# Broadcast rows by transposes instead of products, and products of constants in the waits of two norms

## The chip, the cores and the metric

The kernel runs on one core of one Trainium2 chip. The metric is the device time of one launch in microseconds (us); lower is better. TensorE multiplies matrices into PSUM, VectorE (DVE) and ScalarE (ACT) do the element-wise work, GpSimd (POOL) does a little of it, and SyncE (SP) issues the loads of weights.

## The reference, cut to what matters

A sequence of 512 tokens of width 1024 goes through two blocks, all in float32. The first block is a norm, a projection, banded attention beside a pooling branch, a gated mix, an output projection whose result is normed and added to `x`, and then a convolution-gated feed-forward whose result is normed and added again. The second block is a norm, a projection, four heads of a gated delta rule (chunked recurrence) beside four heads of differential attention, and an output projection.

```python
x = x + rms_norm(mix, norm_mix_post)                       # first norm with a wait
f = conv_gated_ffn(rms_norm(x, norm_ffn_pre), ...)
x = x + rms_norm(f, norm_ffn_post)                         # second norm with a wait
...
g = cumsum(g); decay = exp(where(tril, g[:, None] - g[None, :], -inf))
k_beta = k * beta;  k = k / sqrt(sum(k * k) + eps)
```

In `rms_norm` each token has one factor, and in the delta rule each token of a head has a cumulated log decay `g`, a strength `beta` and a factor of its key's norm. Each of these is a column of numbers (a token per partition) that is also needed as a row (a token per column, the same on all 128 partitions), because activations are stored with features on partitions and the 512 tokens along the free dimension.

## The kernel before, in words

Everything is hand-scheduled: each engine has one program in order, and they meet at semaphores. Weights come in 155 units of 128x1024 through a ring of four buffers. ScalarE rounds a unit to `Wh` (L1697), VectorE takes the rest `Wl` (L1023), and TensorE does three products of 128x512 for each 128x128 piece: `Wh*Hh`, `Wh*Hl`, `Wl*Hh` (L509, L510, L512, and L544 where several units run together behind a norm). These dense products are most of the kernel.

A row is made from four columns (128 tokens each) by four calls on TensorE. The operand `scalars[:, t:t+1]` is one column of four, spread with stride 0 over 128 columns, and is multiplied with the identity, so that each partition of the output gets the same 128 numbers. A float32 product of two operands is issued as two passes, each with its own weight load, so a row of four calls is 8 passes; a call of `pe.transpose` is one pass (the transposes of L753 are 4 passes for four tiles). The rows are:

- `norm_row(turn)` (L576 to L582) for the norms before the first projection (turn 0), the feed-forward (turn 1) and the second block (turn 2);
- the row in `post_norm(turn)` (L592 to L596), for the norm after the mix (turn 0) and after the feed-forward (turn 1);
- three rows for each of the four heads in TensorE's `prep` (L800 on), by `row_of` (L745): "g" and "b" (L806, L807), and "kr", the factors of the keys' norms (L827). For "g" the second operand is an upper triangular matrix in place of the identity, so that the product also cumulates the log decays `glog` of the head; "b" spreads `beta`. Both read `gs`, into which VectorE's `prep` copies them first (L1363, L1364), and TensorE waits for that copy.

`post_norm` is where TensorE waits. All units before it are done; TensorE then waits until ScalarE has squared the last sum (L1816), adds up squares over the partitions with products of one column (L588, L589), VectorE scales the sums (L1081), GpSimd takes the power -0.5 (L2115), TensorE spreads the factors as a row (L594), VectorE scales and adds the first tile of `X` (L1068, L1071), ScalarE makes its rounded part `Hh` (L1711), and VectorE the rest `Hl` (L1037). Then the dense products start again in `units_together` (L544), tile after tile of the eight: four units at once in turn 1, two at once in turn 2, where products of one column (L563) stand between the tiles.

In the second block the order is written as rounds: `second_block` runs four stages, one for each head, in which the preparation of head `a` runs beside the recurrence (`scan`) and the attention (`diff`) of the head before, and dense products of later units (3 at a time) fill in between. All engines walk through the same rounds. At the start of stages 1 to 3, TensorE does the first product of the recurrence (L887), the rows and products of `diff`, the rows "g" and "b", some dense products, and then the second products of the recurrence (L892), which read `head_VN`. VectorE makes that (L1485) behind a copy of a unit (L1023), which waits for ScalarE's rounding (L1697), which stands behind the gate function of that stage (L1889) in ScalarE's order.

Of the kernel before, what the change touches and what calls it, by code (L numbers as in the profile page):

```python
# [18 lines left out]
P = 128  # L19
# [3 lines left out]
NT = S // P  # L23
# [124 lines left out]
def program(nc, ctx, x_in, w_units, w_ba, cols_in, mats_in, rope_in, rows_in, relb_in, counts_in,  # L148
# [7 lines left out]
    def sb(name, shape, dt=F32):  # L156
        t = nc.alloc_sbuf_tensor_at(name, shape, dt, offset=place[0])
        size = 4
        for n in shape[1:]:
            size *= n  # L160
        place[0] += (size + 31) // 32 * 32
        return t
# [93 lines left out]
    St = sb("St", [P, P])  # L256
    gs = sb("gs", [P, 2, NT])
    rqk = sb("rqk", [P, 2 * NT])
# [18 lines left out]
    def steps(name, names):  # L277
        return Steps(nc, ctx, name, names)
# [18 lines left out]
    def sum_read(g):  # L297
# [75 lines left out]
        x for lv in levels for x in (("y", lv), ("t", lv), *(("kt", "qk") if lv == 1 else ()))), "u", "w"])  # L373
    prep_dv = steps("prep_vector", ["gs", "d", "bm", "dt", "ms", "vb", "kn", "lt0", "lt", "strips",
                                    "m0", "tt", "ti", "lm", *(
# [122 lines left out]
    def tensor_program():  # L498
# [77 lines left out]
        def norm_row(turn):  # L576

            pe.wait_ge(*norm_gp.at(turn, "rstd"))
            for t in range(NT):
                ins = pe.matmul(PS[:, 2, tok(t)], rstd[:, t:t + 1].to_broadcast([P, P]), ident[:],  # L580
                                start=True, stop=True)
            ins.then_inc(*norm_pe.tick(turn, "bcast"))  # L582

        def post_norm(turn):
            pe.wait_ge(square_added, (turn + 1) * KT)
            pe.wait_ge(square_done, (turn + 1) * KT)
            for t in range(NT):
                pe.matmul(PS[:, 3, t:t + 1], ssum[:, tok(t)], ones[:], start=True, stop=False)  # L588
                ins = pe.matmul(PS[:, 3, t:t + 1], sq[:, (KT - 1) % 2, tok(t)], ones[:],  # L589
                                start=False, stop=True)  # L590
            ins.then_inc(*post_pe.tick(turn, "cols"))
            pe.wait_ge(*post_gp.at(turn, "rstd"))  # L592
            for t in range(NT):
                ins = pe.matmul(PS[:, 2, tok(t)], rstd[:, t:t + 1].to_broadcast([P, P]), ident[:],  # L594
                                start=True, stop=True)
            ins.then_inc(*post_pe.tick(turn, "bcast"))  # L596

        def attention(i):
# [145 lines left out]

        def row_of(bank, scalars, rhs):  # L745
            for t in range(NT):
                ins = pe.matmul(bank[:, tok(t)], scalars[:, t:t + 1].to_broadcast([P, P]), rhs,
                                start=True, stop=True)
            return ins
# [50 lines left out]
        def prep(st, i):  # L800
            yield
            pe.wait_ge(*prep_dv.at(i, "gs"))
            if i:
                pe.wait_ge(*prep_ac.at(i - 1, "u"))
                pe.wait_ge(*prep_dv.at(i - 1, "wt"))
            row_of(b6, gs[:, 0, :], mat(K_UPPER)).then_inc(*prep_pe.tick(i, "g"))  # L806
            row_of(b7, gs[:, 1, :], ident[:]).then_inc(*prep_pe.tick(i, "b"))  # L807
            yield
# [17 lines left out]
            pe.wait_ge(*decay_ac.at(i, "dt"))  # L826
            row_of(b6, rqk[:, 0:NT], ident[:]).then_inc(*prep_pe.tick(i, "kr"))  # L827
            yield
# [185 lines left out]
    def vector_program():  # L1014
# [344 lines left out]
        def prep(st, i):  # L1359
            dv.wait_ge(*gate_dv.at(0, "beta_eg"))  # L1360
            if i:
                dv.wait_ge(*prep_pe.at(i - 1, "w"))
            dv.tensor_copy(gs[:, 0, :], glog[:, i, :])  # L1363
            dv.tensor_copy(gs[:, 1, :], beta[:, i, :]).then_inc(*prep_dv.tick(i, "gs"))  # L1364
            yield
# [977 lines left out]
```

## Time and profile before

| | |
|---|---|
| median of 3 runs | 1120.34 us |
| the three runs | 1119.86, 1120.34, 1129.06 us |
| the profiled execution, its own time | 1117.23 us |
| its span in the trace | 1115.8 us |
| TensorE busy with products | 1071.8 us, 96% |
| VectorE, ScalarE, GpSimd busy | 649.7, 443.1, 89.8 us |
| TensorE's mean granted clock | 0.983 of full speed |

The profiled execution's span leaves 1.4 us of its own time outside (launch and end). "Idle before" in a row is the time in which the engine had nothing, and the arrow names what ended it. The granted clock has two levels, 1.0 (2.4 GHz) and 0.5 (1.2 GHz); a figure between them is a mean over the stretch.

### The profile page before, as it was taken

What the parts mean: (1) busy time and instruction counts of PE and PEld (TensorE: products, weight loads), DVE (VectorE), ACT (ScalarE), POOL (GpSimd) and SP (SyncE); (2) the same over time, 40 slices, a digit from 0 to 9 for tenths busy, and PEclk for the clock granted to TensorE, in tenths of its full rate; (3) what the DMA queues carried; (4) which work ended last, traced back from release to release, by engine and by line L of the source; (5) the groups of instructions that cost most, each with busy time, mean ns of one, the idle gap of its engine ahead of it and who ended that gap; (6) DMA issues with size and microseconds to landing.
All of it is one profiled execution on the core that took longest, in us unless ns stands there. A gap on an engine that the chain in (4) does not pass through costs nothing.

```text
span 1115.8 us, 15447 instructions
## 1 busy us (share of the span) xinstructions
PE 1071.8 (96%) x6280; PEld 850.5 (76%) x6280; DVE 649.7 (58%) x1126; ACT 443.1 (40%) x773; POOL 89.8 (8%) x76
## 2 busy tenths in 40 slices
PE   7999999999989999999999999889999999998898
PEld 5777777778768888888888888768777777775776
DVE  6645454656337788777772212654576576575474
ACT  6233232344443544444442222434254354353431
POOL 1000000000210000000000000000120120221210
PEclk9999999999989999999999999899999999998899
DMA  8221313122331233333323233122111111111102
GB/s 328 78 89 59 95 57 95 57 76 83 106 94 57 95 113 103 105 95 96 95 93 105 85 114 113 43 73 73 59 53 44 58 57 40 57 38 40 38 19 76
DMA packets 25430, 90.80 MB, mean 81 GB/s; under 512 B 2880, under 2 KB 3136, under 8 KB 25232
## 3 DMA queue, kind: packets, MB, share of 16 engines
q1 hardware_dynamic: 23328, 83.90, 23.7%
q0 software_dynamic: 592, 3.61, 0.8%
q10 hardware_dynamic: 1440, 2.31, 0.6%
q8 instruction: 50, 0.82, 0.3%
q14 instruction: 20, 0.16, 0.0%
HBM read 87.71 MB, written 2.10 MB: 80 GB/s over the span
## 4 chain that ended last, share of the span: by engine, by line
PE 86%; DVE 7%; ACT 3%; issue 2%; POOL 1%; DMA 1%; SPq 0%; ACTq 0%; DVEq 0%; POOLq 0%
PE PS L509 22%; PE PS L512 21%; PE PS L510 21%; PE PS L544 4%; PE PS L758 1%; DVE Wl L1023 1%; PE PS L629 1%; PE PS L996 1%; PE PS L993 1%; PE PS L994 1%; PE PS L642 1%; ACT Wh L1697 1%; DVE Yc L1062 1%; PE PS L940 1%; PE PS L652 1%
## 5 line engine op out<-in xcount | busy, mean ns | idle before, releaser
L509 PE MATMUL PS<-Hh,Wh 128*128 128x512 f32 x856 | 352.0, 411 | 0.6 <-ACT M L1817 0.6
L512 PE MATMUL PS<-Hh,Wl 128*128 128x512 f32 x856 | 336.2, 393 | 0.0
L510 PE MATMUL PS<-Hl,Wh 128*128 128x512 f32 x856 | 336.0, 392 | 0.0
L1023 DVE TENSOR_TENSOR Wl<-raw,Wh 128x1024 fp32r<-128x1024 f32 x155 | 188.9, 1224 | 186.4 <-ACT Wh L1697 184.8
L509 PEld LDWEIGHTS PS<-Hh,Wh 128*128 128x128 f32 x856 | 161.7, 189 | 43.7 <-issue 11.0
L1697 ACT ACTIVATE Wh<-raw 128x1024 fp32r<-128x1024 f32 x155 | 161.4, 1051 | 72.8 <-PE PS L512 60.9
L512 PEld LDWEIGHTS PS<-Hh,Wl 128*128 128x128 f32 x856 | 161.9, 189 | 35.5
L510 PEld LDWEIGHTS PS<-Hl,Wh 128*128 128x128 f32 x856 | 162.2, 190 | 30.2 <-issue 1.4
L509 PE MATMUL PS<-Ah,Wh 128*128 128x512 f32 x176 | 69.8, 396 | 0.0
L510 PE MATMUL PS<-Al,Wh 128*128 128x512 f32 x176 | 69.8, 396 | 0.0
L512 PE MATMUL PS<-Ah,Wl 128*128 128x512 f32 x176 | 69.8, 396 | 0.0
L1816 ACT ACTIVATE sq<-PS 128x512 f32<-128x512 f32 x16 | 9.6, 598 | 88.7 <-PE PS L512 88.7
L544 PE MATMUL PS<-Hh,Wh 128*128 128x512 f32 x72 | 31.8, 442 | 12.4 <-ACT Hh L1711 12.1
L1062 DVE TENSOR_TENSOR tmp<-PS,RB 128x512 f32<-128x512 f32 x44 | 30.3, 691 | 21.1 <-PE PS L512 18.9
L1844 ACT ACTIVATE conv<-conv 128x512 f32<-128x512 f32 x22 | 13.9, 633 | 71.0 <-DVE conv L1265 71.0
L2107 POOL MEMSET ssum<- 128x512 f32 x2 | 1.1, 530 | 482.4 <-DVE Hl L1250 256.0
L512 PEld LDWEIGHTS PS<-Ah,Wl 128*128 128x128 f32 x176 | 33.1, 188 | 8.1
L510 PEld LDWEIGHTS PS<-Al,Wh 128*128 128x128 f32 x176 | 33.1, 188 | 8.1
L509 PEld LDWEIGHTS PS<-Ah,Wh 128*128 128x128 f32 x176 | 33.1, 188 | 8.1
L1831 ACT ACTIVATE conv<-tmp,cols 128x512 f32<-128x512 f32 x44 | 35.2, 802 | 6.0 <-DVE tmp L1062 6.0
L1768 ACT ACTIVATE sq<-sq,nmax 128x512 f32<-128x512 f32 (+3 forms) x32 | 17.7, 554 | 44.8 <-DVE nmax L1188 44.2
L1579 DVE SCALAR_TENSOR_TENSOR C<-Yc,cols,C 128x511 f32<-128x511 f32 (+2 forms) x36 | 26.6, 746 | 12.8 <-ACT C L2023 8.1
(313 smaller groups left out, 1508.6 us busy)
## 6 DMA issues: line engine op xcount, KB each, us to landing
raw<-in_w_units SPq DMA_DIRECT2D x155, 512.0 KB, 3.5
relb<-in_rel POOLq DMA_DIRECT2D x1, 2048.0 KB, 9.5
out<-X ACTq DMA_DIRECT2D x8, 256.0 KB, 2.1
X<-in_x SPq DMA_DIRECT2D x3, 512.0 KB, 8.0
X<-in_x SPq DMA_DIRECT2D x2, 256.0 KB, 4.3
raw<-in_w_units SPq DMA_DIRECT2D x2, 256.0 KB, 4.6
rope<-in_rope POOLq DMA_DIRECT2D x1, 512.0 KB, 4.3
mats<-in_mats POOLq DMA_DIRECT2D x1, 448.0 KB, 3.6
```

The costliest lines, as they stand in the source:

```text
L509: pe.matmul(bank, Wh[:, s, w], rhs[0](r), start=first and j == 0, stop=False)
L510: pe.matmul(bank, Wh[:, s, w], rhs[1](r), start=False, stop=False)
L512: ins = pe.matmul(bank, Wl[:, s, w], rhs[0](r), start=False, stop=last and end)
L544: return pe.matmul(banks[u], w[:, s, own], h[:, k, :], **ends)
L629: pe.matmul(PS[:, 2 + a, 0:nk], Q2[r, tok(qt)], K2[r, 0:nk], start=True, stop=True).then_inc(*att_pe.tick(i, ("scores", n, a)))
L1023: dv.tensor_tensor(Wl[:, s, :], raw[:, s, :], Wh[:, s, :].bitcast(F32), sub).then_inc(unit_split, 1)
L1062: return dv.tensor_tensor(dst, PS[:, bank_of[g], :], RB[:], mult).then_inc(bank_read[g % 2], 1)
L1579: dv.scalar_tensor_tensor(out=c[:, 3 - n:], in0=y[:, 0:S - 3 + n], scalar=col(C_CONV2 + a * 12 + 4 * j + n), in1=c[:, 3 - n:], op0=mult, o ...
L1697: ac.activation(Wh[:, s, :], raw[:, s, :], ACT.Copy).then_inc(unit_rounded, 1)
L1768: ac.activation(w, w, ACT.Exp, bias=nmax[:, b + a:b + a + 1], scale=1.0, accum_out=rsum[:, b + a:b + a + 1]).then_inc(*att_ac.tick(i, ("ex ...
L1831: ac.activation(conv[:, p % 2, j % 2, :], tmp[:, j % 2, :], ACT.Identity, bias=col(C_CONV + 4 * j + 3), scale=col(C_CONV + 4 * j + 2)).the ...
L1844: ac.activation(c, c, ACT.Gelu_apprx_tanh).then_inc(up_gelu, 1)
```

## The change

Five places change. (1) The row in `norm_row` and in `post_norm` is made by `pe.transpose` of the spread column. (2) `row_of` does the same, for all three rows of a head; "g" now reads `gcum`, the cumulated decays that VectorE already has (L1351), and "b" reads `beta` directly. (3) VectorE no longer copies into `gs`, and `gs` and its step are gone; TensorE waits for `beta_eg`, the last step of the gate chain, which runs once before the first head. (4) A new function `keep_awake(n)` issues `n` products of the identity with 256 columns of `cols`, both constants in float32, into bank 5, which nothing reads. (5) `post_norm` calls it three times: 1 product ahead of the wait for the squares, 2 ahead of the wait for the factors, and 5 behind the row.

```diff
-    gs = sb("gs", [P, 2, NT])
...
         def norm_row(turn):
             pe.wait_ge(*norm_gp.at(turn, "rstd"))
             for t in range(NT):
-                ins = pe.matmul(PS[:, 2, tok(t)], rstd[:, t:t + 1].to_broadcast([P, P]), ident[:],
-                                start=True, stop=True)
+                ins = pe.transpose(PS[:, 2, tok(t)], rstd[:, t:t + 1].to_broadcast([P, P]), ident[:])
...
+        def keep_awake(n):
+            for _ in range(n):
+                pe.matmul(PS[:, 5, 0:2 * P], ident[:], cols[:, 0:2 * P], start=True, stop=True)
...
         def post_norm(turn):
+            keep_awake(1)
             pe.wait_ge(square_added, (turn + 1) * KT)
...
             ins.then_inc(*post_pe.tick(turn, "cols"))
+            keep_awake(2)
             pe.wait_ge(*post_gp.at(turn, "rstd"))
             for t in range(NT):
-                ins = pe.matmul(PS[:, 2, tok(t)], rstd[:, t:t + 1].to_broadcast([P, P]), ident[:],
-                                start=True, stop=True)
+                ins = pe.transpose(PS[:, 2, tok(t)], rstd[:, t:t + 1].to_broadcast([P, P]), ident[:])
             ins.then_inc(*post_pe.tick(turn, "bcast"))
+            keep_awake(5)
...
-        def row_of(bank, scalars, rhs):
+        def row_of(bank, columns):
             for t in range(NT):
-                ins = pe.matmul(bank[:, tok(t)], scalars[:, t:t + 1].to_broadcast([P, P]), rhs,
-                                start=True, stop=True)
+                ins = pe.transpose(bank[:, tok(t)], columns[:, t:t + 1].to_broadcast([P, P]), ident[:])
...
-            pe.wait_ge(*prep_dv.at(i, "gs"))
+            pe.wait_ge(*gate_dv.at(0, "beta_eg"))
             if i:
                 pe.wait_ge(*prep_ac.at(i - 1, "u"))
                 pe.wait_ge(*prep_dv.at(i - 1, "wt"))
-            row_of(b6, gs[:, 0, :], mat(K_UPPER)).then_inc(*prep_pe.tick(i, "g"))
-            row_of(b7, gs[:, 1, :], ident[:]).then_inc(*prep_pe.tick(i, "b"))
+            row_of(b6, gcum[:, i, :]).then_inc(*prep_pe.tick(i, "g"))
+            row_of(b7, beta[:, i, :]).then_inc(*prep_pe.tick(i, "b"))
...
-            row_of(b6, rqk[:, 0:NT], ident[:]).then_inc(*prep_pe.tick(i, "kr"))
+            row_of(b6, rqk[:, 0:NT]).then_inc(*prep_pe.tick(i, "kr"))
...
         def prep(st, i):
-            dv.wait_ge(*gate_dv.at(0, "beta_eg"))
-            if i:
-                dv.wait_ge(*prep_pe.at(i - 1, "w"))
-            dv.tensor_copy(gs[:, 0, :], glog[:, i, :])
-            dv.tensor_copy(gs[:, 1, :], beta[:, i, :]).then_inc(*prep_dv.tick(i, "gs"))
             yield
```

## Rows read from the trace of the kernel before

**Rows 1.** The page: the span, TensorE's busy time, and the chain by engine.

```profile
span 1115.8 us, 15447 instructions
...
PE 86%; DVE 7%; ACT 3%; issue 2%; POOL 1%; DMA 1%; SPq 0%; ACTq 0%; DVEq 0%; POOLq 0%
```

**Rows 2.** Timeline, first norm's wait: start us, duration us, engine, line, operation [idle before].

```profile
324.93 0.35 PE L588 MATMUL PS<-ones,ssum 128*128 128x1 f32 x2 [0.78 <-ACT sq L1816]
...
328.21 1.25 PE L594 MATMUL PS<-ident,rstd 128*128 128x128 f32 x8 [1.36 <-POOL rstd L2115]
...
331.92 0.76 PE L544 MATMUL PS<-Hh,Wh 128*128 128x512 f32 x1 [2.46 <-ACT Hh L1711]
...
335.27 0.75 DVE L1037 SCALAR_TENSOR_TENSOR Hl<-X,cols,Hh 128x512 fp32r<-128x512 f32 x1
...
338.02 0.39 PE L544 MATMUL PS<-Hh,Wh 128*128 128x512 f32 x1
```

**Rows 3.** Windows there: us, busy PE PEld DVE ACT POOL, granted clock, DMA.

```profile
326.00:330.00 4.00, 2.10 (x16) 1.73 (x15) 0.66 (x2) 0.31 (x1) 1.02 (x1) 0.89 0.15 61
330.00:335.00 5.00, 3.08 (x7) 2.48 (x8) 4.89 (x8) 2.48 (x4) 0.00 (x0) 0.50 0.00 0
335.00:340.00 5.00, 5.00 (x21) 4.05 (x20) 4.93 (x9) 3.13 (x6) 0.00 (x0) 0.90 0.34 105
```

**Rows 4.** Timeline, second norm's wait.

```profile
703.46 2.08 PE L594 MATMUL PS<-ident,rstd 128*128 128x128 f32 x8 [1.37 <-POOL rstd L2115]
...
708.00 0.76 PE L544 MATMUL PS<-Hh,Wh 128*128 128x512 f32 x1 [2.46 <-ACT Hh L1711]
...
710.33 0.72 ACT L1711 ACTIVATE Hh<-X,cols 128x512 fp32r<-128x512 f32 x1 [0.74 <-DVE X L1071]
...
711.86 0.48 PE L544 MATMUL PS<-Hh,Wh 128*128 128x512 f32 x1
```

**Rows 5.** Windows of the second norm's wait, columns as above.

```profile
700.00:705.00 5.00, 3.63 (x23) 3.54 (x23) 0.16 (x1) 0.24 (x1) 2.04 (x3) 0.62 0.59 210
705.00:710.00 5.00, 2.54 (x8) 1.89 (x8) 4.32 (x7) 2.48 (x4) 0.00 (x0) 0.50 0.00 0
710.00:715.00 5.00, 5.00 (x29) 4.41 (x28) 4.93 (x9) 3.18 (x6) 0.00 (x0) 0.86 0.00 0
```

**Rows 6.** Timeline of TensorE, head 0: four transposes, then a row of products.

```profile
765.89 0.66 PE L753 MATMUL PS<-ident,C 128*128 128x128 f32 x4 [0.16 <-DVE rqk L1382]
766.30 0.48 PE L509 MATMUL PS<-Hh,Wh 128*128 128x512 f32 x1
...
767.78 1.05 PE L747 MATMUL PS<-ident,rqk 128*128 128x128 f32 x8
768.59 0.47 PE L509 MATMUL PS<-Hh,Wh 128*128 128x512 f32 x1
```

**Rows 7.** Timeline at the starts of stages 1, 2 and 3 (heads 1 to 3).

```profile
816.71 0.49 PE L892 MATMUL PS<-head_VN,head_Kd 128*128 128x128 f32 x2 [0.37 <-DVE head_VN L1485]
...
897.40 0.49 PE L892 MATMUL PS<-head_VN,head_Kd 128*128 128x128 f32 x2
...
974.21 1.24 DVE L1363 COPY gs<-glog 128x4 f32<-128x4 f32 x1
...
975.57 1.16 PE L747 MATMUL PS<-mats,gs 128*128 128x128 f32 x8 [0.77 <-DVE gs L1364]
975.78 1.04 ACT L1697 ACTIVATE Wh<-raw 128x1024 fp32r<-128x1024 f32 x1
...
976.85 1.23 DVE L1023 TENSOR_TENSOR Wl<-raw,Wh 128x1024 fp32r<-128x1024 f32 x1 [1.34 <-ACT Wh L1697]
...
978.99 0.49 PE L892 MATMUL PS<-head_VN,head_Kd 128*128 128x128 f32 x2 [0.66 <-DVE head_VN L1485]
```

**Rows 8.** Window of a later stretch with a wait, columns as above.

```profile
1014.00:1020.00 6.00, 3.45 (x77) 2.69 (x78) 3.95 (x13) 1.45 (x7) 0.00 (x0) 0.89 0.00 0
```

**Rows 9.** Timeline in that stretch, TensorE.

```profile
1019.39 0.48 PE L946 MATMUL PS<-ident,head_Wd 128*128 128x128 f32 x1 [2.11 <-DVE head_Wd L1563]
```

More of the change, by code:

```diff
@@ L373, in program @@
         x for lv in levels for x in (("y", lv), ("t", lv), *(("kt", "qk") if lv == 1 else ()))), "u", "w"])
-    prep_dv = steps("prep_vector", ["gs", "d", "bm", "dt", "ms", "vb", "kn", "lt0", "lt", "strips",
+    prep_dv = steps("prep_vector", ["d", "bm", "dt", "ms", "vb", "kn", "lt0", "lt", "strips",
                                     "m0", "tt", "ti", "lm", *(
```

## The prediction

> **What bounds the kernel now.** I read the page first. The reader is to see that the chain which ended last runs through TensorE for 86% of the span [rows 1]: what is taken off TensorE's own program counts in full wherever nothing else is waited for. So I read the timeline at each place that the change touches, for the wait that ends last there, and the windows of the granted clock.
>
> There are two kinds of place. At the two norms with a wait, TensorE stands idle for 0.78, 1.36 and 2.46 us in one passage [rows 2], and the clock falls: it is 0.89 in the window from 326 to 330, 0.50 in the next and 0.90 in the next [rows 3]. So it was at 1.2 GHz for 0.22 x 4 + 5 + 0.2 x 5 = 6.9 us. In the second norm the means are 0.62, 0.50 and 0.86 [rows 5], which is 3.8 + 5 + 1.4 = 10.2 us. The dense products that follow start in that state. At the rows of the second block there is no such passage. There the question is whether TensorE or the chain ScalarE, VectorE is late.
>
> **The change, part by part.** The unit of price is a row. Eight passes take 768.59 - 767.78 = 0.81 us from start to start, four transposes of the same size 766.30 - 765.89 = 0.41 us [rows 6]. A row turned into transposes gives 0.40 us at full clock.
>
> *Rows of the three norms with `norm_row`:* 3 x 0.40 = 1.2 us. VectorE waits for each of these rows, so its reading starts earlier too. I see no wait behind them that another engine alone sets.
>
> *Head 0, rows "g", "b", "kr":* 3 x 0.40 = 1.2 us. The copies into `gs` are not waited for there.
>
> *Row "kr" of heads 1 to 3:* 3 x 0.40 = 1.2 us. It lies on the chain that ended last; if the waits behind it are set by others it is worth nothing, so the bounds are 0 and 1.2, and I take 1.2.
>
> *Rows "g" and "b" of heads 1 to 3, and the copies into `gs`:* here most of the work that is removed is removed from in front of a wait. In head 3 TensorE idles 0.77 us for `gs` at 975.57, whose first copy took 1.24 us; the same in head 2. Then it idles 0.66 us at L892 for `head_VN`. That is made behind ScalarE's rounding at 975.78, and behind VectorE's split at 976.85, which had waited 1.34 us for that rounding [rows 7]. Neither waited for the rows or for `gs`. So L892 stays at 978.99 against the start of the stage, and 0.77 + 0.80 us turn into a wait there. In head 1 L892 had 0.37 us of idle already, and in head 2 it started without one, at 897.40 [rows 7], right behind the vector operation that it reads. Of 2.4 us in rows and about 1.5 us in waits for `gs`, I count 0.1 us. If I am wrong on who is late, up to 3.9 us more are gained.
>
> *The row in `post_norm`:* in the first norm 8 passes took 1.25 us and in the second, with the clock down, 2.08 us [rows 2, 4]. Four transposes take 0.66 us with their latency [rows 6], or twice that cold: 0.6 us gained in the first; in the second 1.0 us when the clock is down as before, 1.4 us when it is up. All that VectorE does for the first tile shifts by as much.
>
> *The products of constants.* The trace before has none. One has two passes of 256 columns, thus 512 columns where the 8 passes of a row have 1024: half of 0.81, or 0.41 us at full clock and 0.82 at half. One product lies in an idle time of 0.78 us; two are 0.82 us in 1.36; five are 2.05 us in 2.46 [rows 2]. All fit at full clock and cost nothing. At half clock the two take 1.64 us and the five 4.1 us: 0.3 + 1.6 = 1.9 us beyond the waits that cover them. Bounds of their own cost: 0 to 1.9 us for each norm.
>
> *What the clock gives, if it stays up.* First norm: the products of L544 before 338.02 start at 331.92 - 0.6 = 331.3. Tile 0 has 6 and tile 1 has 12 of them, 0.23 us each, thus 4.1 us if nothing is waited for, but the last four need the `Hl` that ends at 336.02 [rows 2], now 335.4. So they end at 335.4 + 4 x 0.23 = 336.3 in place of 338.02, which gives 1.7 us with the row's 0.6. From there TensorE is the late one (5.00 of 5.00 us busy [rows 3]). Second norm: tile 1 waits for `Hh`, ready at 710.33 + 0.72 = 711.05, and its products start at 711.86 [rows 4]. At full clock they start when it is ready, 0.8 us earlier, and 1.4 with the row: 2.2 us; a little more, 0.25, since the last of the sums (L588, L589) ran cold as well: 2.5 us.
>
> Will it stay up? The products fill 3.3 of some 7 us in each passage; of the rest nearly half goes to products of one column. That is near the edge: at 1018 the clock fell (0.89 over the window of rows 8, down at its end) in a stretch that ends in 2.11 us of idle, with much small work ahead of it [rows 8, 9]. I expect that it holds in some executions and norms and falls in others, but comes back sooner, as the five products are dense work behind the row. Between the row alone (0.6 and 1.0) and the whole (1.7 and 2.5) I take the middle, 1.2 and 1.8 us.
>
> By the Trainium skill, "TensorE: Matmul & The Clock Gate", section "Terms", a transpose of float32 is four times as fast; the trace has twice (0.81 against 0.41 us [rows 6]), and the sum goes by that. By the factor four, 0.2 us more would go for each of the rows that I count.
>
> *A cost.* In head 3 TensorE now idles longer in front of L892: 0.66 + 0.77 + 0.80 = 2.2 us, with transposes ahead of it. A fall of the clock there would be partly hidden, since TensorE waits for VectorE around it. I put 0.3 us to it as a mean.
>
> The sum: 1.2 + 1.2 + 1.2 + 0.1 + 1.2 + 1.8 - 0.3 = 6.4 us. Against the profiled execution (span 1115.8, its own time 1117.23) that is 1110.8; but that execution is 3.1 us below the median shown and the clock differs from one execution to the next, so I set the sum against the median: 1120.34 - 6.4 = 1113.9 us.
>
> **The rivals.** *The clock falls in both norms all the same.* Then the constants overrun at half clock. For it: the fall in rows 8 and 9. Against it: nothing in the passage is now idle for more than about a microsecond. Each norm then has its row (0.6 and 1.0) less 1.9 us, plus an earlier return of the clock, which gives 0.5 to 1.5 us: about zero. What is left is 1.2 + 1.2 + 1.2 + 0.1 = 3.7: 1116.6 us.
>
> *All works.* The clock holds in both norms (1.7 + 2.5) and no fall is added: 3.7 + 4.2 = 7.9 us, 1112.4 us. With something of the 3.9 us in front of L892 it would come below 1109.
>
> *The rows of the second block are worth nothing*, as ScalarE and VectorE set its pace: only the norms count, 1.2 + 1.2 + 1.8 = 4.2 us, 1116.1 us. For it: the waits of rows 7. Against it: 86% of the chain on TensorE [rows 1].
>
> *Slower: the rows no longer hold the clock in the second block.* At the start of stages 1 to 3 dense float32 products of two passes become transposes, and the waits at L892 grow to 0.37 + 0.8 = 1.2 us, about 1.6 and 2.2 us. If the clock falls in each of them for as long as in the norms (6.9 to 10.2 us, half of which is lost: 3.4 to 5.1 us), that costs 10 to 15 us against a gain of 6.7 without the mean cost above: 1124 to 1129, say 1126. It decides from the second such fall on. Against it: at L892 dense products follow at once, and part of the loss is hidden by VectorE. The Trainium skill says in "TensorE: Matmul & The Clock Gate", section "Part 4: PE-mode transpose", that a transpose does not count as busy for the clock in the way that a product does, which is this mechanism; no row here shows it, since transposes are always among products before.
>
> **How the numbers follow.** Forecast 1113.9: 0.50, its own range 1110.5 to 1117. The clock falls in both norms: 0.20. All works: 0.12, a third of it under 1109. Rows of the second block worth nothing: 0.12. Slower: 0.06. A measurement of this kernel tells about 1% from no change, so faster means below 1109.1 and slower above 1131.5. The tail of the forecast under 1109.1 holds 0.05, all works 0.04 and luck with the falls late in the span (rows 8) 0.02: faster 0.11. Slower than 1131.5 needs the last rival at its dearest: 0.02. The range that holds 8 in 10 is 1108 to 1119.5.
>
> **What would show it.** L594 has 4 instructions for each norm and L747 only 48, at 0.41 us a row. The granted clock in the windows of rows 3 and 5 is at or near 1.0, and L544 starts some 7.1 us behind the last product ahead of the norm, not 8.1. No `gs`; L747 is not waited for, and L892 is idle for more than a microsecond in heads 1 and 3. Wrong would be: L544 starting right behind the last constant product with the clock at 0.5 (overrun); L892 without a longer wait (then more is gained); or a clock under 1.0 between 815 and 985.

## The result, and the profile after

| | before | changed |
|---|---|---|
| median, executions | 1120.34 us, 14 | 1113.45 us, 14 |
| lowest to highest | 1117.13 to 1129.21 | 1110.31 to 1117.39 |
| profiled execution, own time (span) | 1117.23 (1115.8) | 1111.07 (1109.6) |
| mean granted clock of that execution | 0.983 | 0.986 |

The ratio of the times is 0.9905, with a 95% interval of 0.9881 to 0.9929. It stands for 10.6 us, and the means differ by 9.8 us; the medians differ by 6.9 us only, since 5 of the 14 executions of the kernel before took 1128.5 us or more and a median passes them over. The forecast was 1113.9 us and "within 1%"; both came out. The change did what it says: L599, the row in the wait of a norm, has 8 instructions where L594 had 16, the rows of the heads have 48 (L753) where L747 had 96, and `gs` is gone.

The page of the changed kernel, for [rows 1]:

```profile
span 1109.6 us, 15364 instructions
...
PE 86%; DVE 7%; ACT 3%; issue 2%; POOL 1%; DMA 0%; ACTq 0%; DVEq 0%; POOLq 0%
```

The first norm's wait in the timeline of the changed kernel, for [rows 2]; L592, L599 and L543 are L588, L594 and L544 of before, and L585 is the products of constants:

```profile
323.52 0.60 PE L585 MATMUL PS<-cols,ident 128*128 128x256 f32 x2
324.47 0.35 PE L592 MATMUL PS<-ones,ssum 128*128 128x1 f32 x2 [0.34 <-ACT sq L1816]
...
326.24 1.75 PE L585 MATMUL PS<-cols,ident 128*128 128x256 f32 x4
327.79 1.06 PE L599 MATMUL PS<-ident,rstd 128*128 128x128 f32 x4
328.65 2.99 PE L585 MATMUL PS<-cols,ident 128*128 128x256 f32 x10
331.32 0.54 PE L543 MATMUL PS<-Hh,Wh 128*128 128x512 f32 x1
...
335.47 1.19 PE L543 MATMUL PS<-Hl,Wh 128*128 128x512 f32 x4 [0.54 <-DVE Hl L1042]
336.50 0.39 PE L543 MATMUL PS<-Hh,Wh 128*128 128x512 f32 x1
```

And the second norm's, for [rows 4]:

```profile
699.60 1.11 PE L585 MATMUL PS<-cols,ident 128*128 128x256 f32 x4
701.12 0.65 PE L599 MATMUL PS<-ident,rstd 128*128 128x128 f32 x4 [0.40 <-POOL rstd L2115]
701.60 2.32 PE L585 MATMUL PS<-cols,ident 128*128 128x256 f32 x10
704.23 0.47 PE L543 MATMUL PS<-Hh,Wh 128*128 128x512 f32 x1 [0.30 <-ACT Hh L1711]
...
706.64 0.47 PE L543 MATMUL PS<-Hh,Wh 128*128 128x512 f32 x1
```

Windows of both passages in the changed kernel (us, busy PE PEld DVE ACT POOL, granted clock, DMA), for [rows 3, 5]:

```profile
324.00:328.00 4.00, 3.66 (x22) 2.98 (x22) 0.16 (x1) 1.85 (x3) 1.02 (x1) 0.82 0.48 182
328.00:332.00 4.00, 4.00 (x17) 3.45 (x17) 3.04 (x5) 1.57 (x3) 0.00 (x0) 0.75 0.00 0
332.00:336.00 4.00, 3.46 (x15) 2.41 (x14) 3.97 (x6) 2.12 (x4) 0.00 (x0) 1.00 0.39 98
698.00:702.00 4.00, 3.60 (x26) 3.12 (x26) 0.36 (x2) 0.26 (x1) 2.06 (x3) 1.00 0.78 260
702.00:706.00 4.00, 3.70 (x18) 2.67 (x17) 3.90 (x7) 2.49 (x4) 0.00 (x0) 1.00 0.01 2
```

The reader is to see two outcomes of the same remedy in one execution. In the second norm the clock stays at its upper level, and the idle times of 1.37 and 2.46 us have shrunk to 0.40 and 0.30. In the first it still fell, for about 3.4 us (0.82 and 0.75 in two windows of 4 us), so the constants there took 1.75 and 2.99 us in the records; but it was back for the dense products at L543, where before it stayed down 6.9 us. The row there was made with the clock down: it took 1.06 us where the eight passes had taken 1.25, so of the 0.6 us that the row was to give there came 0.1, and the rest of the gain is dense products at the upper level.

Where the 6.2 us came from can be read by laying marks of both traces side by side:

| mark | before | changed | ahead by |
|---|---|---|---|
| first product | 7.16 | 7.87 | -0.7 |
| sums of the first norm (L588, now L592) | 324.93 | 324.47 | 0.5 |
| its tile 1 done (L544, now L543) | 338.02 | 336.50 | 1.5 |
| sums of the second norm | 699.81 | 697.83 | 2.0 |
| its tile 1 begins | 711.86 | 706.64 | 5.2 |
| gate sums (L740, now L745) | 749.81 | 744.09 | 5.7 |
| transposes of head 0 (L753, now L758) | 765.89 | 759.26 | 6.6 |
| L892, now L897, of head 3's stage | 978.99 | 972.35 | 6.6 |
| L786, now L791 | 1007.36 | 1002.38 | 5.0 |
| first L892, now L897, of the last stage | 1055.64 | 1049.53 | 6.1 |

The late first product was made up by 15 us (both kernels then stand at 15.2), so ahead of the first norm only the row of `norm_row(0)` counts, with 0.5 us. The first norm gave 1.0 us and the second 3.2. From head 1 on the lead doesn't grow any more, but it moves:

- each "kr" row of heads 1 to 3 adds 0.4 to 0.6 us (the lead behind it is 7.2 at 835, 6.7 at 916 and 5.0 at 995 us of the kernel before, from 6.7, 6.3 and 4.4);
- rows "g" and "b" and the copies add 0.8 to 2.0 us, and the wait at L897 behind them takes it all back, to within 0.2 us;
- two falls of the clock that the profile of before doesn't have take back 1.0 us (865.9 to 869.3) and 2.2 us (971.7 to 978.5);
- one that both have is shorter in the changed kernel (3.4 us from 1016.1, against 6.8 from 1018.6), which gives 1.2 us.

The waits at L897 (changed kernel, timeline of TensorE at the starts of stages 1 to 3, for [rows 7]):

```profile
809.99 0.49 PE L897 MATMUL PS<-head_VN,head_Kd 128*128 128x128 f32 x2 [1.27 <-DVE head_VN L1485]
...
891.12 0.49 PE L897 MATMUL PS<-head_VN,head_Kd 128*128 128x128 f32 x2 [1.93 <-DVE head_VN L1485]
...
970.09 0.58 ACT L1979 ACTIVATE head_Vdt<-PS 128x512 f32<-128x512 f32 x1
970.21 1.23 DVE L1028 TENSOR_TENSOR Wl<-raw,Wh 128x1024 fp32r<-128x1024 f32 x1 [2.56 <-ACT Wh L1697]
...
972.35 0.80 PE L897 MATMUL PS<-head_VN,head_Kd 128*128 128x128 f32 x2 [2.62 <-DVE head_VN L1485]
```

and the window around the last of them, with the clock at 0.64 on average:

```profile
970.00:976.00 6.00, 3.65 (x10) 2.52 (x11) 5.79 (x9) 2.54 (x4) 1.47 (x2) 0.64 0.31 90
```

VectorE waits 2.56 us for ScalarE's rounding where it waited 1.34 after the copy into `gs`: the rows and the copies were in front of a wait that ScalarE sets. In stage 3 the longer wait of 2.62 us ends with the clock down, and the lead drops from 6.6 to 4.4 us, of which the "kr" row behind it brings 0.6 back.

### The profile page after: what moved, and what is told of

It reads as the page before. It is cut to its first block, busy times and chain, and to the rows that moved or that the text cites. A ratio compares the mean times of both kernels' runs of the same rounds, so it can differ in the third digit from the quotient of the medians.

```text
span 1109.6 us, 15364 instructions
## 1 busy us (share of the span) xinstructions
PE 1070.1 (96%) x6244; PEld 847.8 (76%) x6244; DVE 647.2 (58%) x1118; ACT 443.1 (40%) x773; POOL 89.3 (8%) x76
## 4 chain that ended last, share of the span: by engine, by line
PE 86%; DVE 7%; ACT 3%; issue 2%; POOL 1%; DMA 0%; ACTq 0%; DVEq 0%; POOLq 0%
PE PS L508 22%; PE PS L511 21%; PE PS L509 21%; PE PS L543 5%; PE PS L763 1%; PE PS L634 1%; DVE Wl L1028 1%; PE PS L1001 1%; PE PS L998 1%; PE PS L999 1%; PE PS L647 1%; ACT Wh L1697 1%; PE PS L945 1%; DVE Yc L1067 1%; PE PS L657 1%
## 5 line engine op out<-in xcount | busy, mean ns | idle before, releaser
L543 PE MATMUL PS<-Hh,Wh 128*128 128x512 f32 x72 | 30.1, 418 | 8.2 <-DVE Wl L1133 7.9
```

Of the source, the lines that this page charges most:

```text
L543: return pe.matmul(banks[u], w[:, s, own], h[:, k, :], **ends)
```

## The experiments

Every kernel was timed beside executions of the kernel before on the same chip. The mean granted clock of each execution is given with the times, since it explains most of what follows. A table of 92 executions of the kernel before, all those that ran beside e1, e5, e9 and e12, shows what it is worth:

| mean granted clock | 0.971 | 0.974 | 0.976 | 0.979 | 0.980 | 0.983 | 0.985 |
|---|---|---|---|---|---|---|---|
| executions | 17 | 14 | 4 | 22 | 16 | 6 | 2 |
| mean time, us | 1128.8 | 1126.3 | 1124.7 | 1121.5 | 1120.0 | 1117.0 | 1115.3 |

(The other eleven lie at 0.973, 0.977 and 0.982.) From 0.985 to 0.971 the time at the lower level grows by 0.014 x 2 x 1120 = 31 us and the execution by 13.5 us: 0.43 us for each cold microsecond, or 0.96 us for each 0.001 of the mean. At one clock the executions lie within 2.5 us of each other, against 14.7 us over all, so the spread of this kernel's times goes with the clock. Between two kernels the same table says less, because it matters where the cold time lies: a cold microsecond inside a wait costs little. In the profile of e2, the norms had 10.2 us less of it than in the profile of before (3.4 and 3.4 against 6.8 and 10.2), and that gave 0.1 us in the first and 1.7 in the second.

### e1 and e2: each half of the change alone

e1 leaves out the constants of the changed kernel, e2 adds the constants alone to the kernel before.

```diff
 # e1, on the changed kernel
-            keep_awake(1)
...
-            keep_awake(2)
...
-            keep_awake(5)
```

> The changed kernel without its three calls of products of constants; the rows stay transposes. Theory A (the sum of the prediction, with the second norm's part corrected by the profile after to 3.2 us where the clock holds): the rows outside the two waits give 3.7 us, the rows in the waits 0.6 and 1.0, together 5.3; with one fall of the clock early in stage 3 about 1 us is given back, so 1116 us (ratio 0.996), with the granted clock at 0.5 behind both norms and L543 starting with 0.76 us products. Theory B (the constants do nothing for the time, the clock returns anyway): the same time as the changed kernel, 1113.5 (0.994). Theory C (only the clock mattered, the rows of the second block are worth nothing): 1118 to 1120.

> The kernel before with the products of constants added in the two waits, rows still of two passes. Theory A: 1.1 us in the first norm and about 2.2 us in the second where the clock holds, a little over half of it on average: 1118 us (0.998), no fall or a shorter one in the two norms. Theory B (constants are idle work): 1120.3 (1.000). Theory C (clock is the whole gain): 1115 (0.995). With e1: the two gains should add up to that of the change.

Measured: e1 1122.05 us, ratio 0.9999 (0.9974 to 1.0023); e2 1116.17 us, 0.9955 (0.9925 to 0.9984). The rows alone gave nothing, where 4 us were expected; the constants alone 5 us, 3 more than expected; together 0.9905. The two halves don't add. The clocks say how: the mean over the executions was 0.9729 in e1 and 0.9780 in the kernel before beside it. By the table 0.005 is 4.9 us, just what the rows should have gained; and at the same clock, 0.976, e1 took about 1119.8 us (2 executions) where the kernel before took 1124.7. So the rows take some 5 us of work off, as the terms of the prediction had it (3.7 + 0.6 + 1.0 = 5.3), and in e1 the lower clock took it back. With the constants it is the other way round: at the same clock, 0.985, e2 took 1117.7 us (2 executions) and the kernel before 1115.3, and at 0.983 it was 1119.7 (1) and 1117.0 (6). So e2 is faster by its higher clock alone (a mean of 0.986), and 2.4 to 2.7 us go back, as cold time that was cheap, or as constants that are not wholly covered. The second is seen in its profile: the clock fell ahead of the first norm's row, and tile 0 began at 332.94 right behind the last constant, 0.8 us later against the sums than before (timeline of e2; in the kernel before tile 0 began at 331.92 [rows 2]):

```profile
325.13 0.35 PE L594 MATMUL PS<-ones,ssum 128*128 128x1 f32 x2 [0.34 <-ACT sq L1824]
...
330.27 2.86 PE L587 MATMUL PS<-cols,ident 128*128 128x256 f32 x10
332.94 0.47 PE L544 MATMUL PS<-Hh,Wh 128*128 128x512 f32 x1
```

The clearest view of what the constants do comes from the falls of the clock at the two norms, counted over all profiles but that of e6:

| kernels | norms with a fall | how long the clock was down at each |
|---|---|---|
| no constants: before, e1, e5, e9, e10 | 10 of 10 | 6.8 to 10.2 us in the first norm, 10.2 to 20.5 in the second |
| all constants (e8 as transposes): changed, e2, e3, e4, e8, e11, e12 | 9 of 14 | 3.4 us |
| the five behind the row alone: e7 | 2 of 2 | 3.4 and 6.8 us |

So in none of these seven profiles do they keep the clock up in both norms, but where it falls it is back when the dense products begin.

One of the two longest is in e1, in these windows behind its second norm.

```profile
698.00:702.00 4.00, 1.98 (x17) 1.86 (x16) 0.16 (x1) 1.18 (x2) 2.63 (x4) 0.90 0.51 168
702.00:706.00 4.00, 1.40 (x5) 1.03 (x6) 2.64 (x5) 1.24 (x2) 0.08 (x1) 0.50 0.23 94
706.00:710.00 4.00, 4.00 (x15) 3.42 (x14) 3.93 (x8) 2.48 (x4) 0.00 (x0) 0.50 0.00 0
710.00:714.00 4.00, 4.00 (x14) 3.42 (x15) 3.93 (x7) 2.48 (x4) 0.00 (x0) 0.50 0.00 0
714.00:718.00 4.00, 4.00 (x14) 3.42 (x14) 3.93 (x7) 2.50 (x5) 0.00 (x0) 0.50 0.00 0
718.00:722.00 4.00, 4.00 (x16) 3.42 (x16) 3.16 (x4) 3.12 (x4) 0.00 (x0) 0.54 0.00 0
```

TensorE is busy in 4.00 of 4.00 us and still at 0.50. It stayed there from 701.2 to 721.7, 20.5 us. The timeline of e1 shows what it was busy with (L562 is the sums of squares, one column each):

```profile
708.41 1.70 PE L562 MATMUL PS<-ones,up_squares 128*128 128x1 f32 x8
709.97 0.77 PE L543 MATMUL PS<-Hh,Wh 128*128 128x512 f32 x1
...
712.68 1.70 PE L562 MATMUL PS<-ones,up_squares 128*128 128x1 f32 x8
714.24 0.77 PE L543 MATMUL PS<-Hh,Wh 128*128 128x512 f32 x1
```

A tile takes 714.24 - 709.97 = 4.27 us here; warm, in the changed kernel, it takes 2.28. Each tile done cold costs 2 us, and with this mixture of six dense products and eight of one column the clock didn't come back for nearly four tiles. The same mixture doesn't always do so: in the profile of before it was back at 711.4, 3.4 us behind the start of tile 0 [rows 4, 5].

### e3 and e4: the wait in front of L897

e3 makes rows "g" and "b" of heads 1 to 3 by products again; e4 puts constants into that wait.

```diff
 # e4, on the changed kernel (TensorE's prep)
+            for _ in range((0, 4, 7, 10)[i]):
+                pe.matmul(b6[:, 0:P], ident[:], cols[:, 0:P], start=True, stop=True)
             row_of(b6, gcum[:, i, :]).then_inc(*prep_pe.tick(i, "g"))
```

> The changed kernel with rows g and b of heads 1 to 3 made by products of two passes again (6 rows, 0.40 us each, 2.4 us of TensorE's time). Theory A: they lie in front of a wait that VectorE and ScalarE set, so the idle time at L897 (1.27, 1.93 and 2.62 us in the profile of the changed kernel) shrinks by 0.8 each and the time stays: within 0.5 us of the changed kernel (1113.5). If the longer idle time is what makes the clock fall in stage 3, it may even be 0.5 to 1 us faster. Rival: the rows are on the path, 2.4 us slower, 1115.9.

> The changed kernel with 4, 7 and 10 products of constants of 128 columns (0.2 us each) ahead of row g in heads 1, 2 and 3, so that TensorE no longer idles at L897. Theory A (the idle time in front of L897 lets the clock fall in stage 3, which cost 1.7 us in the profile of the changed kernel): no fall at that place in any profile, 1 to 1.5 us faster than the changed kernel, 1112.2. Rival D (that fall is hidden by VectorE or hits anyway): same as the changed kernel, 1113.5. Rival E (the constants delay the rows, which VectorE waits for): slower by up to 1 us.

Measured: e3 1114.03 us, 0.9915 (0.9880 to 0.9950); e4 1113.83 us, 0.9907 (0.9870 to 0.9944), both as the changed kernel. The intervals alone are too wide for the 2.4 us of TensorE's work that e3 puts back (that of e3 spans 8 us), but its timeline shows where it goes. Laid beside the changed kernel, e3 falls behind by 0.9 to 1.0 us at the two rows of each head and has made it up at L904, to within 0.02 us in all three heads. So that the six rows lie in front of a wait that others set is shown. The idle time moved as told (timeline of e3, heads 2 and 3; L904 is L897):

```profile
895.94 0.49 PE L904 MATMUL PS<-head_VN,head_Kd 128*128 128x128 f32 x2 [1.03 <-DVE head_VN L1492]
...
977.18 0.49 PE L904 MATMUL PS<-head_VN,head_Kd 128*128 128x128 f32 x2 [1.71 <-DVE head_VN L1492]
```

Neither profile has a fall at that place, but the medians did not move by the 1 to 1.5 us that I gave to it. Both have other falls that the changed kernel lacks (3.4 us at 724 and 6.8 at 772), so a fall that is gone in one place is not a gain over many executions; how often the one in stage 3 happens is not known.

### e5 and e6: the sums of one column moved

```diff
 # units_together, for the last norm
-                if squares is not None and m < KT:
-                    pe.wait_ge(*norm_sq.at(turn, m))
...
+            if squares is not None:
+                pe.wait_ge(*norm_sq.at(turn, KT - 1))
+                for m in range(KT):
+                    for t in range(NT):
...
```

> The kernel of e1 (rows transposed, no constants) with the 32 sums of squares of the last norm (one column each, L562) moved from between the tiles of units_together behind the last tile; the same instructions, another order. Theory F (behind the second norm the clock stays down for tile after tile, 20.5 us in the profile of e1, because products of one column lie between the tiles; a cold tile takes 4.3 us and a warm one 2.3): the clock comes back within two windows of about 5 us of the first dense products, and the time falls by 4 to 6 us against e1, to 1117 (ratio 0.996). Rival G (the long stretch is chance, or set by the wait alone): as e1, 1122 (1.000).

> The changed kernel with the same move of the sums. Theory F: where the constants hold the clock there is no long cold stretch left to cure, so the slower executions (1116 to 1117) go and the median falls by at most 1 us: 1113 (0.990). Rival G: no difference at all, or slower by up to 1 us, as the last sums are no longer spread.

Measured: e5 1121.18 us, 0.9992 (0.9966 to 1.0018); e6 1120.69 us, 0.9982 (0.9959 to 1.0006). (One execution of e6, the profiled one, took 1506 us at a mean clock of 0.65; it is left out of the ratio and its profile isn't used.) The time was a miss, and the mechanism isn't shown. In the profile of e5 the clock was back at 711.5 in the third tile, 10.2 us after its fall and not 20.5, as Theory F wants it. But the kernel before has its sums between the tiles, and its profile shows 10.2 us as well; e10, which is the kernel before at that place, shows 17.1. So rival G, chance, stands. What e5 does show is a new place to lose time: now all the sums stand together, and the clock falls in them (timeline of e5):

```profile
711.31 0.48 PE L543 MATMUL PS<-Hh,Wl 128*128 128x512 f32 x1
...
720.53 9.44 PE L562 MATMUL PS<-ones,up_squares 128*128 128x1 f32 x64
731.31 1.12 PE L578 MATMUL PS<-ident,rstd 128*128 128x128 f32 x4 [1.34 <-POOL rstd L2093]
```

TensorE was busy all through it. The block took 9.44 us where 64 passes took 8 x 0.81 = 6.5 between the tiles of the changed kernel. It was cold from 725.1 for another 10.2 us. Also, nothing covers this block: it stands whole between the last tile and the norm's chain. e6 shows the cost of that in the changed kernel, which had no long stretch to cure: 7 us slower by the medians (on another chip), where I expected at most 1.

### e7 and e8: which of the constants, and whether transposes do as well

```diff
 # e7: without keep_awake(1) and keep_awake(2)
 # e8, in keep_awake
-                pe.matmul(PS[:, 5, 0:2 * P], ident[:], cols[:, 0:2 * P], start=True, stop=True)
+                for t in range(4):
+                    pe.transpose(PS[:, 5, tok(t)], cols[:, 0:P], ident[:])
```

> The changed kernel with only the five products of constants behind the row; the one and the two ahead of it are left out. Theory F: the clock falls in most executions, since the waits ahead of the row are empty again, but the five are dense work that brings it back before or soon after the tiles begin: most of the gain is kept, 1115 (0.992). Rival H (the fall itself must be avoided): the five run cold (4.1 us in a wait of 2.5), the clock stays down behind the second norm as in e1, 1121 (0.999).

> The changed kernel with each product of constants (2 passes of 256 columns) replaced by four transposes of 128 columns, the same time on TensorE. If transposes count for the clock as products do: 1113.5 (0.991) and clocks as in the changed kernel. If they don't, as the Trainium skill says: the clock falls as in e1 and they run cold beside it, 1121 to 1123 (1.000).

Measured: e7 1115.02 us, 0.9935 (0.9907 to 0.9963), clocks 0.979 to 0.986, close to Theory F: the five behind the row keep 7 of the 10.6 us. In its profile the clock fell in both norms and the five ran cold, in the second for 4.28 us in the records, so tile 0 began right behind them at 705.67 without idle time; but the clock was back by then (705.7), and the tiles ran warm. The three ahead of the row were not tried alone. e8 1112.61 us, 0.9925 (0.9898 to 0.9953), clocks 0.982 to 0.988 with a mean of 0.9847, against 0.984 in the changed kernel. Transposes of constants do as well for the clock as products: in its profile too the clock held in the first norm and fell for 3.4 us in the second, as in e3 and e4. In this kernel the statement of the Trainium skill ("TensorE: Matmul & The Clock Gate", "Part 4: PE-mode transpose") that they don't count as busy in the same way is not borne out, and the measurement decides.

### e9 and e10: which rows give the gain back

e9 turns only the five rows of norms into transposes, e10 only the twelve of the heads; both on the kernel before, without constants.

> The kernel before with only the five rows of norms (L580, L594) made by transposes; the rows of the heads stay products, gs stays. e1 showed that all rows together are worth nothing without the constants, with a mean granted clock of 0.973 in every execution against 0.978 before. Theory J (it is the rows in the norms' waits that give the gain back: TensorE has less to do there, the clock falls sooner and stays down longer behind the second norm): no faster than before or slower, 1121 to 1124 (1.000 to 1.002), clock near 0.973. Theory K (it is given back in the second block): 2.8 us faster in work, 1119 (0.9975), clocks spread as before (0.971 to 0.985).

> The kernel before with only the twelve rows of the heads made by transposes and gs gone; the rows of the norms stay products, no constants. Theory J: the gain of the heads' rows is kept, 2.5 us: 1119.2 (0.998). Theory K (the longer waits at L892 make the clock fall in the second block): as before or slower, 1121.7 to 1123 (1.000 to 1.001). With e9 it shows which half gives the gain back.

Measured: e9 1120.18 us, 0.9970 (0.9946 to 0.9994), mean clock 0.9787; e10 1122.05 us, 0.9989 (0.9966 to 1.0013), mean clock 0.9754; the kernel before beside them 0.9769. Theory J isn't borne out: the rows of the norms keep their gain: 3.4 us by the ratio, and 1.9 us at the same clock, 0.979 (1119.6 us in five executions against 1121.5), for 2.8 expected. The rows of the heads at the same clock, 0.976, take 1121.6 us (eight executions), 3.1 us less than the 1124.7 of the kernel before, but the mean clock is 0.0015 lower, which is 1.4 us, and the interval includes no gain. At the same clock the halves add up, 1.9 + 3.1 = 5.0 us, as much as e1 has; it is the clock that differs. So the loss would lie more with the heads' rows, which is Theory K; but the two intervals overlap, and neither half alone has the clock of e1 (0.9729), so it may need both. Where in the span is not settled. The profiles don't tell it clearly: both have long stretches behind the second norm (20.5 us in e9, 17.1 in e10 by the granted clock), e10 one more fall at 733.9, at a row that it did not change, and the last fall is 13.7 us long in e10, 10.2 in e9. e10 changes nothing on TensorE ahead of 750 us, so that its stretch behind the second norm is longer than in the profile of before is chance, and the same may hold for the 20.5 us of e9 and e1. Single profiles can't settle it.

### e11 and e12: filling the other waits

```diff
 # e11, on e4: first in diff, ahead of the wait for head_Wd; then in pair_norms, ahead of that for sq
+                    pe.wait_ge(*diff_ac.at(i, ("out", n - 2) if n > 1 else "vt"))
+                    if i == GH - 2 and n == NT:
+                        for _ in range(9):
+                            pe.matmul(PS[:, B_PT, 0:P], ident[:], cols[:, 0:P], start=True, stop=True)
                     pe.wait_ge(*diff_dv.at(i, ("w", n - 1)))
-                    pe.wait_ge(*diff_ac.at(i, ("out", n - 2) if n > 1 else "vt"))
...
-            pe.wait_ge(*qk_ac.at(i, "Qb"))
...
+            if i == GH - 1:
+                for _ in range(8):
+                    pe.matmul(bank[:, 2 * P:3 * P], ident[:], cols[:, 0:P], start=True, stop=True)
+            pe.wait_ge(*qk_ac.at(i, "Qb"))
```

In both places another wait was moved as well, so that the one that is to be filled comes last; the order of the work is the same. e12 adds 5 products of 128 columns ahead of the last norm's factors and 9 ahead of `glog`.

> The kernel of e4 (constants also ahead of row g) with two more fills in the last stage: 9 products of constants of 128 columns ahead of the wait for head_Wd (2.11 us idle at L951 in the profile of the changed kernel) and 8 ahead of the wait for sq in pair_norms (1.94 us idle at L877). In the profile of the changed kernel the clock is down for 3.4 us from 1016 and 10.2 us from 1029.7. If filled waits hold the clock there as they do in the norms: no fall between 1010 and 1045 in the profile, mean clock 0.990 or more, and at 0.4 us for each cold microsecond 4 to 5 us faster than e4: 1109 (0.987). If the falls there come from the small products of the inverses and not from the waits: as e4, 1113.8 (0.991).

> The kernel of e11 with two more fills of constants: 5 products of 128 columns ahead of the wait for the last norm's factors (1.34 us idle at L579) and 9 ahead of the wait for glog (2.27 us idle at L745). In the profile of e11 the clock still falls at 744.6 for 3.4 us. If what e11 showed holds here too, that fall goes: 1 to 1.5 us faster than e11, 1105.5 (0.985). If that fall comes from other work, or costs nothing because VectorE sets the pace there: as e11, 1106.7 (0.986). If the constants overrun their waits: up to 1 us slower, 1107.7.

Measured: e11 1106.69 us (1104.46 to 1108.24), 0.9861 (0.9829 to 0.9894), every execution at a clock of 0.991 or more. The windows of stage 3, first in the changed kernel:

```profile
965.00:1050.00 85.00, 74.29 (x661) 57.22 (x661) 49.35 (x112) 41.76 (x86) 16.15 (x11) 0.88 0.12 38
```

and in e11:

```profile
965.00:1050.00 85.00, 79.55 (x752) 62.27 (x750) 54.68 (x122) 42.27 (x86) 21.04 (x14) 1.00 0.12 40
```

The clock went from 0.88 to 1.00 for the price of constants that fill two waits (in both TensorE goes from the last constant to the next product with next to no idle time). Of the three falls that the changed kernel has there (971.7, 1016.1 and 1029.7) none is left, and beside the changed kernel e11 gains 5.0 us between 1016 and 1040. e4 with the fills of the rows alone gave nothing and has the two later falls, so it is the two late fills together that do it; neither was tried alone. With e12 this is the fastest version of the study, with 0.6% less than the changed kernel by the medians (on another chip) and 0.4% by the ratios to the kernel before.

e12 1106.79 us (1101.53 to 1109.86), 0.9831 (0.9798 to 0.9864). Its ratio is lower, but the kernel before had lower clocks beside it (a mean of 0.9755 against 0.9769, median 1125.98); the medians of e11 and e12 are equal. The fall at 744.6 was gone from its profile, another stood at 770.6. A gain from more constants there can't be seen in six executions.

## Why the prediction was right, point by point

The sum was 6.4 us, the profiled executions differ by 6.2 and the medians by 6.9. That the totals agree so well is partly luck: two terms were off by 1.4 and 1.6 us and cancel. By the lead of the changed kernel in the two profiles:

| term | predicted | in the profiles |
|---|---|---|
| three rows of `norm_row` | 1.2 | 1.4 |
| head 0 | 1.2 | 1.3 |
| "kr" of heads 1 to 3 | 1.2 | 1.5 |
| "g", "b" and `gs` of heads 1 to 3 | 0.1 | -0.3 |
| first norm | 1.2 | 1.1 |
| second norm | 1.8 | 3.2 |
| falls of the clock in the second block | -0.3 | -1.9 |

Term by term:

- *A row gives 0.40 us.* In the changed kernel a "kr" row takes 0.36 us from start to start (761.15 to 761.51) where it took 0.81: 0.45. Right.

```profile
761.15 0.60 PE L753 MATMUL PS<-ident,rqk 128*128 128x128 f32 x4
761.51 0.48 PE L508 MATMUL PS<-Hh,Wh 128*128 128x512 f32 x1
```

- *Rows of the norms with `norm_row` and of head 0.* The lead grows by about 0.5 us at each of the three norms' rows, by 0.9 at "g" and "b" of head 0 and by 0.4 at its "kr". Right. e9 agrees for the five rows of norms.
- *Row "kr" of heads 1 to 3: 1.2 us, with bounds of 0 and 1.2.* 0.5, 0.4 and 0.6 us. Right: no wait took it.
- *"g" and "b" of heads 1 to 3 and `gs`: 0.1 of 3.9 us.* The three waits took back all and 0.3 us more. Right, and shown by the timeline of e3. The predicted waits at L892, 1.2, 1.6 and 2.2 us, came out as 1.27, 1.93 and 2.62.
- *The constants cost nothing where the clock holds, and the first norm gives 1.2.* It gave 1.0 to 1.1 us, with the clock down for half as long as before.
- *The second norm gives 1.8, at most 2.5.* It gave 3.2 in the profile, where the clock held. The bound was mis-sized: I took the `Hh` at 710.33 for tile 1's, but it is tile 2's; tile 1's was ready 2 us sooner, so the products of tile 1 had no such wait. (A slip in the same term did no harm: the row with the clock down was to gain 2.08 less twice 0.66, which is 0.8 and not 1.0 us; but four cold transposes take 1.11 us, as in e1, which does give 1.0.) On average over executions the term may be worth more still, since the profile of before was a mild one: 1117.23 us at 0.983, where 61 of the 92 executions in the table were at 0.979 or less. In which place those have their cold time isn't known.
- *0.3 us for a fall in head 3.* It took 2.2 us in the profile of after, and one more fall in head 2, which no term had, 1.0 us; 1.2 us came back at 1018, where the fall was shorter than before. By e4 the one in head 3 costs less than can be measured on average.

Of the signs that the prediction named, some failed. The granted clock was at 1.0 in the second norm only. L543 came 8.0 us behind the last product ahead of the first norm and not 7.1 (in the second it is 7.6 where it was 9.4). And "a clock under 1.0 between 815 and 985", named as a sign of being wrong, came out: its mean there is 0.96, with falls at 865.9, 947.8 and 971.7. That sign couldn't have told much, since the profile of before has a fall at 953.8 and a mean of 0.99 in the same stretch.

What the prediction had wrong is that it added the halves up. The rows were to be worth 3.7 us outside the waits whatever the constants did, which was also the time of the first rival, 1116.6. e1 measured that case without constants: nothing. The total came out because the constants gave more (5 us in e2, where my terms for the two norms hold 3.0 - 0.6 - 1.0 = 1.4 us for the clock) and kept what the rows would have lost. So the mechanism "the constants hold the clock through the waits, or bring it back sooner" carried nearly the whole, and the lighter rows paid only together with the constants. Why they lower the clock without them, in which places and by which of them, stays open. The slower rival, in which the lighter rows let the clock fall in the second block, was priced too high, but a lower clock with the rows alone is in e1 and, less surely, in e10: it takes back 5 us in e1 and 1.4 in e10. That it happens at L892, as that rival had it, is not shown.

## What to carry to other kernels

When TensorE is the bound and its clock has two levels, count the cold microseconds of many executions before anything else: here one cost 0.43 us on average between executions of one kernel, and a spread of 13 us went with it. Products of constants that just fill a wait (length of the idle time divided by the measured time of one product) gave 0.5% at the norms and a further 0.4 to 0.6% in the last stage. They cost nothing where the clock holds; where it falls all the same they run at half speed and overrun the wait, by 0.8 us in e2. The five right ahead of the dense work gave 0.65% by themselves. Taking work off TensorE alone can cost as much clock as it saves time, as in e1, so try such a change together with the fills.

## What the runs showed of the hardware

- A TensorE that is busy in every microsecond can stay at 1.2 GHz: in e1 for 16.0 us (705.7 to 721.7, of 20.5 in all), on six dense products and eight of one column for each tile.
- At the waits of the two norms the clock fell in all ten cases without constants, for 6.8 to 20.5 us, and in 9 of 14 with all of them, for 3.4 us each.
- The sums in one block let the clock fall while TensorE was never idle (e5, from 725.1).
- Transposes of float32 as constants did as well for the clock as products (e8), and four transposes of 128x128 take less than half the time of four products (0.36 against 0.81 us).
- VectorE's copy of 128x4 into `gs` took 0.16 us in two heads and 1.24 us in the other two, where it ended together with a tensor operation of GpSimd that ran beside it. What joins the two was not tried.
